# Inversion of the triangular blocks in a recurrent mixer: products spread over four quadrants of the array, transposed inverse by a product with the identity

## The chip, the cores and the metric

The kernel runs on one core of a Trainium2 chip. The metric is the device time of one launch in microseconds (us). Engines are named as the profile names them: PE (TensorE), ACT (ScalarE), DVE (VectorE), POOL (GpSimd), SP (SyncE). PSUM is the memory that PE writes, eight banks of 128 partitions by 512 fp32 numbers (`k.ps`).

## The reference, cut to what matters

The kernel computes two blocks of a network over 512 tokens. All that the change touches is inside one part of the second block, the two-directional recurrence

```
def rwkv7_scan(r, w, k, v, kk, a, reverse):
    def step(state, inp):
        sa = einsum('bhij,bhj->bhi', state, -kk_t)
        state = (state * w_t[:, :, None, :] + sa[..., None] * (kk_t * a_t)[:, :, None, :]
                 + v_t[..., None] * k_t[:, :, None, :])
        y_t = einsum('bhij,bhj->bhi', state, r_t)
```

which runs forwards and backwards for eight heads of 64 channels. The kernel does it by chunks of 64 tokens. Inside a chunk the removals (`sa`) of later tokens depend on those of earlier ones, so that a unit triangular 64x64 matrix has to be inverted for every chunk, head and direction: 8 x 8 x 2 = 128 inversions.

## The kernel before, in words

Inputs are laid out with channels or tokens on the 128 partitions. Large projections are split into high and low parts and multiplied 128x128 by 512 columns; they fill most of the time. `stage_rw_heads` (L2608) is the stage of the change. It makes four passes (`for c in range(RW_T)`), each for two heads, which lie in the lower and upper 64 partitions while channels are on the partitions. A pass does, on PE in program order: scores (L2736, 64 channels times 128 columns), transposes (`turn`, L2758), products of the scores with the values (L2788), two products for the decays and rates of the next pass (`lora`, L2711), a product of `off` with the identity that gives the transposed first level (L2799), the inversion (L2693), the inverse times `rhs` (L2833), products with `wu` (L2842, L2848, L2857, L2869), a recurrence over the eight chunks (L2879), and the output (L2892).

While tokens are on the partitions, chunk `2*it + par` stands in half `par` of the partitions (0 to 63 or 64 to 127), and a unit `u = 8*d + 4*hd + it` names direction `d`, head `hd` and pair of chunks `it`. So each tensor of the inversion (`T`, `Tt`, `Z`, `off`, 16 units of 64 columns, both halves) holds 32 matrices, 16 for each direction.

The inversion doubles the size of inverted blocks in five levels (`lv` 1 to 5; level 0 is `off` plus the identity). `T` is the inverse so far, `Tt` its transpose, and a level is, for each direction `d`:

- Z: `Z` = (score matrix) times `T`, PE; then ACT copies it out of PSUM (L2937).
- T: `Tt` times `Z`, PE; then DVE writes it into `T` where the level's mask is set (`copy_predicated`, L3130). Level 5 has none.
- Tt: `Z` times `Tt`, PE; then DVE writes it into `Tt` under the other mask (L3130).

Each of these is one call of `tiles64`, here called a product: 16 matrix multiplications of 64x64 by 64 columns into one bank. Input half and output half of the partitions are the same (`h` twice), so they use two of the four 64x64 quadrants of the array in turn. An fp32 multiplication leaves two records in the trace, so that a product has 32. A pass has 28 products. Product number `op` goes to bank `op % 8` and waits until the bank's last content is read.

The order of the work around the inversion is that of the loops, one queue for each engine, with semaphores between them (`past(engine, name, c, n)` waits for count `n` of pass `c`). Three things share the queues with it. On ACT, after the Z copy of direction 1 at levels 3, 4 and 5, three, three and four exponentials of the next pass are computed (`rw_exponentials`; the first waits for `sums`, which DVE makes at level 3); in pass 3, which has no next pass, ACT converts a weight block at level 2 (`split_hi`, L248). On DVE, ahead of the copies of each level, there is: at level 1 the centring and squaring of the pass before (`rw_spread`, L2600 to L2605, not in pass 0) and the decay scans of the next pass (`rw_scans`, L2591); at levels 2 to 5 the next pass's sums, rates and keys; in pass 3 `split_lo` (L257) at level 3. In pass 0 the attention branch's output is transposed, scaled and split among the products (`attention_turned`, `attention_high`, `attention_low`).

```
for op, (name, lv, d) in enumerate(ops):
    ...
    tiles64(pe, bank_of(op), lhs, x, d).then_inc(...)
```

## Time and profile before

| | us |
|---|---|
| median of three runs | 1899.15 |
| lowest and highest | 1898.04, 1901.95 |
| profiled execution, its time | 1899.53 |
| profiled execution, its span | 1897.8 |
| inversions, passes 0 to 3, start to the next stage's product | 29.8, 26.5, 26.6, 26.6 |

The span runs from the first to the last recorded instruction. A timeline row has the start and the length of a run of equal instructions; a matrix multiplication's record lasts about 0.22 us here although the next may start sooner, so the spacing of starts tells the rate and the length of a merged row includes one record's tail. Idle time and its releaser stand in brackets. A window row has, for each engine, the busy time in that window, and PE's granted clock as a share of 2.4 GHz.

### The profile page before, as it was taken

How to read it: one execution, taken by the hardware profiler on the slowest of the kernel's cores; microseconds unless marked ns; L12 is line 12 of the kernel's file. 1: busy time of each engine (PE TensorE's matmuls, PEld its weight loads, DVE VectorE, ACT ScalarE, POOL GpSimd, SP SyncE). 2: the span in 40 equal slices, each digit the busy share in tenths (PEclk: the TensorE clock that was granted, in tenths of full speed). 3: DMA queues.
4: the chain of work that ended last, by engine and by line, in shares of the span. 5: the costliest groups of instructions: out<-in, count | busy, mean ns of one | idle time of the engine just before them, and what ended most of it. 6: DMA issues, size and time to landing. Idle time of an engine off the chain costs nothing. (4 is left out here: it accounts for less than half of the span.)

```text
span 1897.8 us, 36848 instructions
## 1 busy us (share of the span) xinstructions
PE 1823.5 (96%) x15870; PEld 1485.6 (78%) x15870; DVE 1092.1 (58%) x1642; ACT 674.3 (36%) x1098; POOL 312.7 (16%) x296
## 2 busy tenths in 40 slices
PE   7999999999999788999999899999999999999997
PEld 6877757688888667778888669888978888888886
DVE  4665354554257788444366887787574635354545
ACT  4334332332223577442222374433233322122342
POOL 4210011130002665310021340000001000000011
PEclk9999999999999899999999999999999999999998
DMA  5334323142223110224331100002042222322231
GB/s 191 103 108 136 137 83 133 45 189 102 90 74 111 35 38 11 73 89 140 131 102 56 49 1 4 4 3 70 4 178 92 104 104 89 111 89 89 78 100 45
DMA packets 42848, 160.87 MB, mean 85 GB/s; under 512 B 5312, under 2 KB 14528, under 8 KB 28096
## 3 DMA queue, kind: packets, MB, share of 16 engines
q1 hardware_dynamic: 28480, 143.84, 22.2%
q10 hardware_dynamic: 14208, 14.68, 2.2%
q8 instruction: 126, 2.06, 0.5%
q14 instruction: 34, 0.28, 0.0%
HBM read 140.42 MB, written 16.78 MB: 83 GB/s over the span
## 5 line engine op out<-in xcount | busy, mean ns | idle before, releaser
L257 DVE TENSOR_TENSOR wlo<-raw,whi 128x2048 fp32r<-128x2048 f32 (+2 forms) x113 | 251.1, 2222 | 179.0 <-ACT whi L248 178.7
L248 ACT ACTIVATE whi<-raw 128x2048 fp32r<-128x2048 f32 (+2 forms) x113 | 209.1, 1850 | 321.4 <-PE ps L283 161.3
L281 PE MATMUL ps<-act_hi,whi 128*128 128x512 f32 x616 | 243.4, 395 | 0.0
L301 PE MATMUL ps<-act_lo,whi 128*128 128x512 f32 x632 | 240.9, 390 | 0.0
L283 PE MATMUL ps<-act_hi,wlo 128*128 128x512 f32 x616 | 240.7, 391 | 0.0
L282 PE MATMUL ps<-act_lo,whi 128*128 128x512 f32 x616 | 240.4, 390 | 0.0
L300 PE MATMUL ps<-act_hi,whi 128*128 128x512 f32 x592 | 235.5, 398 | 0.0
L305 PE MATMUL ps<-act_hi,wlo 128*128 128x512 f32 x632 | 156.5, 389 | 0.0
L301 PEld LDWEIGHTS ps<-act_lo,whi 128*128 128x128 f32 x632 | 118.7, 188 | 25.3 <-issue 1.2
L305 PEld LDWEIGHTS ps<-act_hi,wlo 128*128 128x128 f32 x632 | 118.6, 188 | 24.6
L300 PEld LDWEIGHTS ps<-act_hi,whi 128*128 128x128 f32 x592 | 111.1, 188 | 32.2 <-issue 8.1
L281 PEld LDWEIGHTS ps<-act_hi,whi 128*128 128x128 f32 x616 | 116.3, 189 | 24.4 <-issue 0.5
L283 PEld LDWEIGHTS ps<-act_hi,wlo 128*128 128x128 f32 x616 | 116.1, 188 | 24.5
L282 PEld LDWEIGHTS ps<-act_lo,whi 128*128 128x128 f32 x616 | 116.3, 189 | 24.1 <-issue 0.5
L3443 PE MATMUL ps<-f_hi,whi 128*128 128x512 f32 x256 | 99.6, 389 | 0.0
L3444 PE MATMUL ps<-f_lo,whi 128*128 128x512 f32 x256 | 99.6, 389 | 0.0
L3445 PE MATMUL ps<-f_hi,wlo 128*128 128x512 f32 x256 | 99.6, 389 | 0.0
L1838 POOL TENSOR_SCALAR att_p<-att_p,small 128x512 f32<-128x512 f32 (+3 forms) x64 | 81.9, 1280 | 52.1 <-DVE small L2005 51.1
L1938 ACT ACTIVATE att_p<-ps,small 128x512 f32<-128x512 f32 (+3 forms) x128 | 66.3, 526 | 28.5 <-DVE small L1982 28.2
L3477 DVE TENSOR_TENSOR xT<-xT,ps 128x512 f32<-128x512 f32 x32 | 22.0, 686 | 82.6 <-PE ps L3445 82.6
L3412 ACT ACTIVATE f_hi<-ff_sq 128x512 fp32r<-128x512 f32 x32 | 20.2, 633 | 123.1 <-DVE ff_sq L3468 123.1
L355 POOL TENSOR_TENSOR norm_ple_total<-norm_ple_total,norm_ple_sq 128x512 f32<-128x512 f32 x6 | 7.8, 1295 | 332.0 <-ACT norm_ple_sq L341 332.0
(552 smaller groups left out, 3478.0 us busy)
## 6 DMA issues: line engine op xcount, KB each, us to landing
raw<-stream_in SPq DMA_DIRECT2D x107, 1024.0 KB, 4.8
v_scratch<-v_out ACTq DMA_DIRECT2D x16, 256.0 KB, 3.3
z_scratch<-zt ACTq DMA_DIRECT2D x16, 256.0 KB, 3.0
mlh_v<-v_scratch SPq DMA_DIRECT2D x4, 1024.0 KB, 4.8
mlh_z<-z_scratch SPq DMA_DIRECT2D x16, 256.0 KB, 2.6
cmp_w<-cmp_w_in SPq DMA_DIRECT2D x2, 2048.0 KB, 11.3
z_scratch<-in_zt ACTq DMA_DIRECT2D x16, 256.0 KB, 3.0
mix_g<-z_scratch SPq DMA_DIRECT2D x16, 256.0 KB, 6.7
```

The source lines that it names most:

```text
L248: act.activation(k.whi[b % 2][:, 0:n], k.raw[b % RAW_SLOTS][:, 0:n], ACT.Copy).then_inc(k.hi_done, 1)
L257: dve.tensor_tensor(k.wlo[b % 2][:, 0:n], k.raw[b % RAW_SLOTS][:, 0:n], k.whi[b % 2][:, 0:n].bitcast(F32), ALU.subtract).then_inc(k.lo_don ...
L281: pe.matmul(bank, hi, x_hi, start=(x == 0), stop=False)
L282: pe.matmul(bank, hi, x_lo, start=False, stop=False)
L283: last = pe.matmul(bank, lo, x_hi, start=False, stop=(x == end))
L300: pe.matmul(bank, hi, x_hi, start=(x == 0), stop=False)
L301: pe.matmul(bank, hi, x_lo, start=False, stop=False)
L305: last = pe.matmul(bank, lo, x_hi, start=False, stop=(x == end))
L1838: pool.tensor_scalar(p[:, m % DEEP, 0, 0:L], p[:, m % DEEP, 0, 0:L], sm(32, m)[:, 0:1], None, ALU.mult) \
L3443: pe.matmul(k.ps[:, t % 4, :], whi, f_hi[:, kt, :], start=(kt == 0), stop=False)
L3444: pe.matmul(k.ps[:, t % 4, :], whi, f_lo[:, kt, :], start=False, stop=False)
L3445: last = pe.matmul(k.ps[:, t % 4, :], wlo, f_hi[:, kt, :], start=False, stop=(kt == KD - 1))
```

## The change

Three things change together in the recurrent mixer.

First, the layout. For the products of the inversion the matrices are addressed in one of two ways, `straight` (half is the chunk's parity `par`, as before) and `crossed` (half is `x`, another bit of the chunk's number). A product reads one kind and writes the other, so that its input half and output half take all four combinations, and the four combinations follow one another (`quarters`). It writes two banks, one for each input half. So that `x` and `y` fall where this needs them, the chunks of the features `ar` are stored in another order (`in_time`, `halves_together`, `place`), and several reads and writes have rearranged access patterns.

Second, `Tt` is no longer kept by a product `Z` times `Tt` and a masked copy. After each level `T` is multiplied by the identity with `T` as the stationary operand (step "R"), which gives its transpose, and ACT copies that out. At level 0 the identity times `off` goes through PSUM and DVE adds the identity, in place of a DVE addition in SBUF during the scores (L3069).

Third, the order: R(0) for both directions, then per level Z, Z, R of the level before (from level 2 on), T, T, and at the end R(5) twice: 32 products in a pass. A product waits for the reader of the one four places before it. The products after the inversion (`rhs` with `Tt`) and L2788 take rows and columns by the new places too. In the diff below the last four pieces are L2788, PE's waits (`q` is the number of the product), ACT's queue (where the exponentials still follow the Z copy of direction 1, ahead of the R copies) and DVE's.

```diff
+def in_time(a):
+    return a.rearrange("p (x m n) -> p x m n", x=2, m=4)
+def halves_together(a):
+    return a.rearrange("p (m x n) -> p x m n", x=2, m=4)
...
+    def steps_of(c):
+        out = [("R", 0, 0), ("R", 0, 1)]
+        for lv in range(1, LEVELS):
+            out += [("Z", lv, d) for d in range(2)]
+            if lv > 1:
+                out += [("R", lv - 1, d) for d in range(2)]
+            out += [("T", lv, d) for d in range(2)]
+            if c == 0 and lv < final:
+                out.append(("A", lv - 1, 0))
+        return out + [("R", final, d) for d in range(2)]
...
+    def straight(par, y, x):
+        return rows_half(par), 4 * (y // 2) + 2 * x + y % 2
+    def crossed(par, y, x):
+        return rows_half(x), 2 * y + par
+    def quarters(pe, name, lv, d, bank):
+        for y in range(4):
+            for other in range(2):
+                for source in range(2):
+                    par, x = (other, source) if name == "T" else (source, other)
+                    sh, su = straight(par, y, x)
+                    ch, cu = crossed(par, y, x)
+                    su, cu = 8 * d + su, 8 * d + cu
+                    if name == "T":
+                        to, h, lhs, y_in = sh, ch, Tt[ch, cu, :], Z[ch, cu, :]
+                    elif name == "Z":
+                        to, h, lhs, y_in = ch, sh, sc[sh, su, 0, :], T[sh, su, :]
+                    elif lv:
+                        to, h, lhs, y_in = ch, sh, T[sh, su, :], eye64[sh]
+                    else:
+                        to, h, lhs, y_in = ch, sh, eye64[sh], off[sh, su, :]
+                    last = pe.matmul(k.ps[to, bank + source, chunk(y)], lhs, y_in, start=True, stop=True)
...
-                    last = pe.matmul(k.ps[h, d, chunk(u % 8)], sc[h, u, 2, :], vtok[h, it, chunk(hd)], start=True,
-                                     stop=True)
+                    last = pe.matmul(k.ps[rows_half(it // 2), par, chunk(4 * d + 2 * hd + it % 2)], sc[h, u, 2, :],
+                                     vtok[h, it, chunk(hd)], start=True, stop=True)
...
+                    if name == "Z":
+                        past(pe, "t", c, made("T", lv - 1, d))
+                    elif name == "T":
+                        past(pe, "zc", c, made("Z", lv, d))
+                        past(pe, "rt", c, made("R", lv - 1, d))
+                    elif name == "R":
+                        past(pe, "t", c, made("T", lv, d)) if lv else past(pe, "off0", c, d + 1)
+                    if q == 1:
+                        past(pe, "t", c, 2)
+                    elif q in (2, 3) and c + 1 < RW_T:
+                        past(pe, "sigs", c + 1, 2 * q - 2)
...
+                    if name == "R" and lv:
+                        past(act, "rz", c, made(name, lv, d))
+                        act.activation(by_pair(Tt, d), from_pair(two), ACT.Copy).then_inc(ss["rt"], 1)
                     if name == "Z":
+                        past(act, "z", c, made(name, lv, d) + 2)
+                        act.activation(by_pair(Z, d), from_pair(two), ACT.Copy).then_inc(ss["zc"], 1)
...
-                past(dve, "off0", c, d + 1)
-                dve.tensor_tensor(units(Tt, d), units(off, d), eye, ALU.add).then_inc(ss["t"], 1)
...
+                    if name == "R" and lv == 0:
+                        past(dve, "rz", c, made(name, lv, d))
+                        dve.tensor_tensor(by_pair(Tt, d), from_pair(two), eye, ALU.add).then_inc(ss["rt"], 1)
                     if name == "Z":
                         if d == 0 and lv == 1 and c:
                             rw_spread(k, dve, steps, c - 1, sqr)
...
+                    if name == "T":
+                        past(dve, "tz", c, made("Z", lv, d))
+                        past(dve, "t", c, made("T", lv - 1, d))
+                        dve.copy_predicated(by_time(T, d), level_mask(lv, 1 - d).bitcast(U32),
+                                            two[:, :, 0:256].rearrange("p a (h m) -> p a h m", h=2)).then_inc(ss["t"], 1)
```

## Rows read from the trace of the kernel before

**Rows 1.** Page: busy us, share of the span and instructions of each engine.

```profile
PE 1823.5 (96%) x15870; PEld 1485.6 (78%) x15870; DVE 1092.1 (58%) x1642; ACT 674.3 (36%) x1098; POOL 312.7 (16%) x296
```

**Rows 2.** Windows: from:to, length, busy (count) of PE, PEld, DVE, ACT, POOL, clock, DMA.

```profile
1140.75:1170.55 29.80, 29.55 (x913) 28.36 (x912) 22.22 (x31) 14.75 (x26) 0.00 (x0) 1.00 0.02 5
1206.62:1233.11 26.49, 26.39 (x897) 26.25 (x897) 22.81 (x30) 12.01 (x22) 0.00 (x0) 1.00 0.02 5
...
1328.86:1355.47 26.61, 26.61 (x897) 26.39 (x897) 17.23 (x23) 7.77 (x11) 0.00 (x0) 1.00 0.02 4
```

**Rows 3.** Groups by line, 1100 to 1375 us: busy, mean ns, idle before, releaser.

```profile
L2937 ACT ACTIVATE rw_Z<-ps 128x512 f32<-128x512 f32 x40 | 23.9, 597 | 59.2 <-PE ps L2693 59.2
```

**Rows 4.** Timeline of PE in pass 1: start, length in us, instruction, idle before it.

```profile
1190.49 1.15 PE L2892 MATMUL ps<-rw_state,rw_ar 64*64 64x64 f32 x62 [0.46 <-DVE rw_state L3170]
...
1191.91 0.45 PE L2736 MATMUL ps<-rw_ar,rw_bt 64*64 64x128 f32 x8
1192.13 0.45 PE L2736 MATMUL ps<-rw_ar,rw_kt 64*64 64x128 f32 x8
...
1198.77 2.08 PE L2788 MATMUL ps<-rw_vtok,rw_sc 64*64 64x64 f32 x64
...
1212.27 2.03 PE L2693 MATMUL ps<-rw_T,rw_sc 64*64 64x64 f32 x64
1214.13 1.10 PE L2693 MATMUL ps<-rw_Z,rw_Tt 64*64 64x64 f32 x32
...
1233.11 0.27 PE L2833 MATMUL ps<-rw_rhs,rw_Tt 64*64 64x128 f32 x1
...
1237.90 0.27 PE L2848 MATMUL ps<-rw_tok,rw_wu 64*64 64x64 f32 x2
```

**Rows 5.** Timeline of DVE in pass 1.

```profile
1205.43 0.67 DVE L2600 TENSOR_REDUCE small<-rw_ytok 128x8 f32<-128x512 f32 x1
...
1208.52 2.34 DVE L2591 TENSOR_TENSOR_SCAN rw_X<-consts,rw_sig 128x512 f32<-128x512 f32 x2
1210.77 0.71 DVE L3130 COPY_PREDICATED rw_T<-rw_consts,ps 128x512 f32<-128x512 uint32 x1
1211.37 0.72 DVE L3130 COPY_PREDICATED rw_Tt<-rw_consts,ps 128x512 f32<-128x512 uint32 x1
...
1236.86 0.69 DVE L3137 COPY rw_wu<-ps 128x512 f32<-128x512 f32 x1 [0.93 <-PE ps L2833]
```

**Rows 6.** Timeline of ACT in pass 1.

```profile
1213.41 0.60 ACT L2937 ACTIVATE rw_Z<-ps 128x512 f32<-128x512 f32 x1 [4.07 <-PE ps L2693]
...
1220.56 1.28 ACT L2565 ACT_TABLE_LOAD   x1
...
1222.91 0.20 ACT L2573 ACTIVATE rw_pend<-rw_X 128x8 f32<-128x8 f32 x1
...
1226.04 0.62 ACT L2578 ACTIVATE rw_X<-rw_X 128x512 f32<-128x512 f32 x1
...
1227.08 0.62 ACT L2565 ACTIVATE rw_ar<-rw_X 128x512 f32<-128x512 f32 x1
```

**Rows 7.** Timeline of ACT in pass 3.

```profile
1337.08 1.90 ACT L248 ACTIVATE whi<-raw 128x2048 fp32r<-128x2048 f32 x1
```

**Rows 8.** Windows before, in and after stretches in which TensorE had little to do.

```profile
1075.70:1079.10 3.40, 0.07 (x2) 0.07 (x2) 2.91 (x6) 1.57 (x5) 2.78 (x3) 1.00 1.03 424
1079.10:1082.50 3.40, 3.40 (x8) 1.04 (x8) 3.33 (x5) 1.22 (x4) 3.26 (x4) 0.50 0.22 94
1249.80:1253.20 3.40, 2.03 (x78) 1.61 (x80) 1.07 (x6) 0.55 (x1) 0.00 (x0) 1.00 0.02 5
1311.20:1314.60 3.40, 2.02 (x57) 1.45 (x59) 1.15 (x7) 0.60 (x1) 0.00 (x0) 1.00 0.70 213
1314.60:1318.00 3.40, 3.40 (x96) 3.40 (x90) 1.19 (x3) 0.00 (x0) 0.00 (x0) 0.50 1.01 360
```

**Rows 9.** Timeline of PE at the start of pass 3.

```profile
1316.35 0.75 PE L2736 MATMUL ps<-rw_ar,rw_bt 64*64 64x128 f32 x8
```

More of the change, by code:

```diff
@@ L2638, in stage_rw_heads, with made, pair_of @@
     final = LEVELS - 1
-    ops = []
-    for lv in range(1, LEVELS):
-        ops += [("Z", lv, d) for d in range(2)]
-        for d in range(2):
-            ops += ([("T", lv, d)] if lv < final else []) + [("Tt", lv, d)]
-    made = {("Tt", 0, 0): 1, ("Tt", 0, 1): 2, ("T", 0, 0): 3, ("T", 0, 1): 4}
-    for x in ops:
-        if x[0] == "Z":
-            made[x] = 2 * (x[1] - 1) + x[2] + 1
-        else:
-            made[x] = 5 + sum(y in made and y[0] != "Z" for y in ops)
-    all_made = made["Tt", final, 1]
+    def steps_of(c):
[8 more added lines that the diff above has]
+        return out + [("R", final, d) for d in range(2)]
+    def made(name, lv, d):
+        return (2 * lv if name in "RT" else 2 * (lv - 1)) + d + 1
+    def pair_of(q):
+        n = 2 * (0, 2, 1, 3)[q % 4]
+        return n, k.ps[:, n:n + 2, :]
     each, ss = RW_EACH, k.rw_ss
@@ L2686, in v_of @@
         return k.rw[:, 8 + c, :]
-    def tiles64(pe, out, lhs, x, d):
-        for i in range(8):
-            for par in range(2):
-                h = rows_half(par)
-                last = pe.matmul(out[h, chunk(i)], lhs[h, 8 * d + i, :], x[h, 8 * d + i, :], start=True, stop=True)
+    def straight(par, y, x):
[19 more added lines that the diff above has]
+                    last = pe.matmul(k.ps[to, bank + source, chunk(y)], lhs, y_in, start=True, stop=True)
         return last
@@ new lines, in _ @@
+                    if q == 1:
+                        past(pe, "t", c, 2)
+                    elif q in (2, 3) and c + 1 < RW_T:
+                        past(pe, "sigs", c + 1, 2 * q - 2)
+                    elif q >= 4:
+                        held, at, side = order[q - 4]
+                        if held == "A":
+                            pe.wait_ge(daa["y_lo"], at + 1)
+                        else:
+                            past(pe, {"Z": "zc", "T": "t", "R": "rt"}[held], c, made(held, at, side))
@@ new lines, in _ @@
+                    bank, _ = pair_of(q)
+                    if name == "A":
+                        attention_turned(lv, bank)
+                    else:
+                        quarters(pe, name, lv, d, bank).then_inc(ss[{"Z": "z", "T": "tz", "R": "rz"}[name]], 1)
+                for d in range(2):
+                    past(pe, "rt", c, made("R", final, d))
+                    for y in range(4):
+                        for par in range(2):
+                            for x in range(2):
+                                h, u = crossed(par, y, x)
+                                last = pe.matmul(k.ps[rows_half(par), 2 * d + x, chunk2(y)], Tt[h, 8 * d + u, :],
+                                                 rhs[h, 8 * d + u, :], start=True, stop=True)
+                                if y == 3 and par == 1:
+                                    last.then_inc(ss["wum"], 1)
@@ L2831, in _ @@
+                places = [(d, hd, it, 8 * d + 4 * hd + it) for d in range(2) for hd in range(2) for it in range(TT)]
+                for d, hd, it, u in places:
+                    if hd == it == 0:
+                        past(pe, "wu_a", c, d + 1)
+                        past(pe, "wu_d", c, d + 1)
                     for par in range(2):
                         h = rows_half(par)
-                        last = pe.matmul(k.ps[h, u // 4, chunk2(u % 4)], Tt[h, u, :], rhs[h, u, :], start=True, stop=True)
@@ L2834, in _ @@
-                    if u % 4 == 3:
-                        last.then_inc(ss["wum"], 1)
-                places = [(d, hd, it, 8 * d + 4 * hd + it) for d in range(2) for hd in range(2) for it in range(TT)]
-                for d, hd, it, u in places:
-                    if it == 0:
-                        past(pe, ("wu_a", "wu_d")[hd], c, d + 1)
-                    for par in range(2):
-                        h = rows_half(par)
-                        last = pe.matmul(k.ps[rows_half(hd), 4 + par, chunk(4 * d + it)], wu[h, u, 0:64], sc[h, u, 1, :],
+                        last = pe.matmul(k.ps[rows_half(hd), 4 + par, chunk(4 * d + 2 * (it % 2) + it // 2)], wu[h, u, 0:64], sc[h, u, 1, :],
@@ L2945, in _ @@
                                 x()
-                for g in (0, 2):
-                    past(act, "wum", c, g + 1)
-                    act.activation(wu[:, 4 * g:4 * g + 4, :].rearrange("p u t -> p (u t)"), k.ps[:, g, :], ACT.Copy) \
+                for d in range(2):
+                    past(act, "wum", c, 2 * d + 1)
+                    act.activation(by_time(wu, d)[:, 0], k.ps[:, 2 * d, :].rearrange("p (h m) -> p h m", h=2), ACT.Copy) \
                         .then_inc(ss["wu_a"], 1)
@@ L3099, in _ @@
                         .then_inc(ss["t"], 1)
-                n = 0
-                for op, (name, lv, d) in enumerate(ops):
-                    if c == 0 and op in (9, 11, 13, 15):
-                        attention_low((op - 9) // 2)
+                for q, (name, lv, d) in enumerate(steps_of(c)):
+                    bank, two = pair_of(q)
+                    if name == "A":
+                        attention_low(lv, bank)
+                    if name == "R" and lv == 0:
+                        past(dve, "rz", c, made(name, lv, d))
+                        dve.tensor_tensor(by_pair(Tt, d), from_pair(two), eye, ALU.add).then_inc(ss["rt"], 1)
                     if name == "Z":
```

101 lines of the change are left out of this document (41 added, 60 removed).

## The prediction

> **What bounds the kernel now.** The first thing to read is the page's line of busy times: PE is busy for 96% of the span [rows 1]. A share over the whole program says little about one stage, so next I read windows around the four inversions. They last 29.8 us in pass 0 and 26.5, 26.6 and 26.6 us after it, and PE is busy in all of that while DVE is busy for 17 to 23 us and ACT for 8 to 15 [rows 2]. Third, the groups by line: in front of its 40 Z copies ACT was idle for 59.2 us, and PE's products ended all of it [rows 3]. So today readers wait for PE and PE for nobody: the inversion is bound by the issue of products. Fourth, the timeline: two products (64 records) start at 1212.27 and the next at 1214.13, so one takes 0.93 us [rows 4]; 28 of them make 26.0 us, and a level of six 5.6 us. The reader of the first product starts at 1213.41 [rows 6], 1.14 us after its start, which is 0.21 beyond its issue.
>
> **The price of a product over four quadrants.** The new order of quadrants isn't foreign to this trace. In the output product L2892, input and output halves vary together over all four: 62 records last 1.15 us, without the last one's tail 0.93 us, or 0.06 us for four [rows 4]. The scores (128 columns) start 8 records each 0.22 us [rows 4]. `tiles64` issues two in 0.06. I take half of 0.93, that is 0.47 us for a product, and 0.68 from its start to its reader's, 0.05 more where PE was idle. Bounds: 0.45, and 0.93 if the overlap fails.
>
> This is also where a rule of the Trainium skill speaks against the change. "TensorE: Matmul & The Clock Gate" (section "Wait — 56ns, not 53.3ns?") says that starts of matmuls never come closer than about 25 ns, however few columns. By it 32 records would take an estimated 0.80 us, not 0.47. The 62 records of L2892 came at 15 ns each on average [rows 4], so the trace disagrees with it here; what it would make of the time stands with the third rival.
>
> **PE's work** therefore falls from 28 x 0.93 = 26.0 to 32 x 0.47 = 15.0 us in a pass, 44 us over four. I don't forecast that, because the copies then come on the path. I follow one level of direction 0 from the start of its T copy on DVE. Prices: DVE copies last 0.73 and start 0.60 apart [rows 5]; an ACT copy lasts 0.60 [rows 6] and the next starts 0.5 later; PE starts about 0.05 after either.
> - T copied 0.73, Z(0) starts 0.79; T of direction 1 is copied at 1.33, Z(1) starts 1.39, R(0) 1.92 behind it on PE.
> - R(0)'s reader starts 2.60, copied 3.20. T(0) starts 3.25, its reader 3.98.
>
> So a bare level takes **4.0 us** against 5.6. Two kinds of other work come on top.
>
> *ACT.* The exponentials of the next pass stand after Z(1)'s copy and ahead of R(0)'s, which T(0) now waits for. Z(1)'s copy lets ACT go at 2.6, when R(0) is ready, so they add in full. Level 3: table load to the short one, 1220.56 to 1223.1, 2.55 us. Level 4: three, 0.52 apart, 1.56. Level 5: three and a short one, 1.87 [rows 6]. In pass 3 the weight block takes 1.8 at level 2 [rows 7]. Today all this lies beside PE's products.
>
> *DVE at level 1.* Counted from R(0,0)'s start, DVE's two additions run 0.68 to 1.9. Only behind them come centring (1205.43 to 1208.52, 3.09) and scans (to 1210.77, 2.25) [rows 5], and then T's copy: 7.2 us. Today centring starts while PE still works on `lora` and Z. In pass 0 there is no centring: 1.9 + 2.25 = 4.15. In pass 3 there are no scans, but R(0,1) waits 0.3 for T: 5.2. At the other levels DVE's 1.4 to 1.9 us fit between its copies, except that in pass 0 `attention_low` stands ahead of the sums and makes level 3 1.1 longer.
>
> After the T copy of level 5: 0.73, R's product 0.79 with its start, ACT 0.60 and 0.05, 2.2 us in all.
>
> | pass | levels 1 to 5, end | sum | now | difference |
> |---|---|---|---|---|
> | 0 | 4.15, 4.0, 7.7, 5.6, 5.9, 2.2 | 29.5 | 29.8 | -0.3 |
> | 1, 2 | 7.2, 4.0, 6.6, 5.6, 5.9, 2.2 | 31.5 | 26.5 | +5.0 each |
> | 3 | 5.2, 5.8, 4.0, 4.0, 4.0, 2.2 | 25.2 | 26.6 | -1.4 |
>
> In pass 3 another 0.9 goes, since the first product no longer waits for both T additions. Sum: +7.4.
>
> **Around the inversion.** L2788 (64 records, 2.08 us [rows 4]) now changes its output half every four multiplications, like L2892: half of 1.87, -0.93 a pass, -3.7. From the first L2833 to the first L2848 is 4.8 us now [rows 4]. After: direction 1's products start 0.93 behind, 1.15 to their reader, 0.69 for the copy [rows 5], then 0.35 as now (1237.55 to 1237.90): 3.1, or -1.7 a pass, -6.8. POOL's `mt`, which also waits for the last L2833, is needed only behind two more products on PE and stays hidden. The DVE addition taken out of the scores (0.7, twice a pass) I cost at nothing: PE has transposes and L2788 ahead of it there; uncovered it would be worth at most 1.2 a pass. Copies from two banks and rearranged chunks of 64 columns: no row has the same pattern; nearest, ACT copies 0.60 [rows 6], masked copies 0.72 [rows 5]. Between 0 and +0.1 for each of the ten on a pass's path, at most +4, and -0.02, -1; I take 0.
>
> So far: +7.4 - 3.7 - 6.8 = **-3.1 us**.
>
> **The clock.** After a window with PE busy for 0.07 of 3.4 us the granted clock was 0.50, that is 1.2 GHz; after one with 2.02 busy (57 records) it fell too, after one with 2.03 (78 records) it didn't [rows 8]. The inversion never idles today. Afterwards PE waits 4.7 us at level 1 of passes 1 and 2 (T(1)'s issue ends at 3.3, Z starts at 8.0), 3.0 us at level 3 of both, 4.0 at level 3 of pass 0, and about 2 at eight other levels. I expect six falls. At the low clock eight score records last 0.75 us [rows 9] against 0.45 [rows 4]; the starts are twice as far apart. With Z, Z and R in front of R's copy a level's head then loses 1.4, T another 0.4; a fall that begins inside the idle time costs less. 1.3 each, **+8**, with bounds 0 (no fall) and +15 (eight at 1.8).
>
> **Total.** -3.1 + 8 = +4.9 on the profiled execution's 1899.5 (0.4 above the median): **1904 us**.
>
> **Rivals.**
> - *The clock holds.* In a bare level PE still issues for 2.8 of 4.0 us, and one window of the recurrence with 2.03 busy held [rows 8]. Then -3.1: 1896 us. Against it: PE is idle for 4 to 5 us in three places, and after the one window of such idleness in the rows the clock was at half.
> - *The other work doesn't stand in the way*, the opposite sign. If ACT and DVE reach the R and T copies on time, a pass is 3.0 + 4 x 4.0 + 2.2 = 21.2 against 26.5, with the gains around it -7.9, four passes -32: 1868 us. It decides if exponentials or scans finish before the next product's result is there. ACT's idle time of 59.2 us speaks for it; the order of the two queues, fixed in the program, against it.
> - *The rate of starts is the limit, not the quadrants*, so that a product stays at 0.93 us. Then R(0) is read at 3.8 in its level, T(0) at 5.6, as now, and ACT, free at 3.4, adds 2.1, 1.1 and 1.4 at levels 3 to 5. Level 1 takes 8.0 and the end 2.6: passes 1 and 2 come to 8.0 + 5.6 + 7.7 + 6.7 + 7.0 + 2.6 = 37.6, +11 each. In the same way pass 0 is +6 and pass 3 +5, nothing is won around them, and the time is 1899.5 + 33 = 1932 us. Against it: L2892 [rows 4]. By the rule of the page named above (0.80 us for a product) it would be an estimated 1916 us.
> - *The clock is low for most of the inversions*, twelve falls or one that holds: +18 - 3.1, 1914 us.
>
> **How the numbers follow.** Forecast 0.42, clock holds 0.24, other work out of the way 0.12, no faster starts 0.09, low clock for long 0.13. The likeliest is 1904, by itself 1899 to 1909. A measurement here tells 0.2% from nothing, 3.8 us: the same is 1895.35 to 1902.95. Of the forecast 0.27 lies above and 0.15 inside; slower 0.27 + 0.09 + 0.13 = 0.49. Clock holds: 0.15 inside, 0.09 below; same 0.30, faster 0.09 + 0.12 = 0.21. The range leaves out the 1868 and the 1932 of two rivals (0.21 between them, but part of the second's way to it lies inside) and holds the other three: 1893 to 1914.
>
> **What would show it.** L2693's successor: 32 records with 0.47 us between the starts of two queued products (else the third rival). DVE's scans ahead of the first T copy of passes 1 and 2, with Z of level 2 about 8 us after the first R. ACT's R(2) copy right behind the short exponential, PE waiting for ACT at levels 3 to 5. Inversions of about 31.5 us in passes 1 and 2, longer than now, and 25 in pass 3, plus the clock's part. Granted clock 0.50 inside the inversions. The prediction is wrong if bare levels aren't near 4.0 us, or if the clock stays at 1.00.

## The result, and the profile after

| | us |
|---|---|
| before, median of four runs beside the changed kernel | 1898.65 (1898.04 to 1901.95) |
| after, median of four | 1921.32 (1917.83 to 1923.13) |
| ratio, 95% interval | 1.0114 [1.0095, 1.0132] |
| profiled execution after, span | 1919.1 |

The change makes the kernel 22.7 us slower. 1904 was forecast, 1893 to 1914 as the range: right in direction, wrong by 17 us. In the table of the experiments the time of e4_split is that of one run, since its other one (2047.05 us) was in the chip's slower state, with a mean granted clock of 0.965 against 0.989. The page's line of busy times, which answers to [rows 1]:

```profile
PE 1801.5 (94%) x16382; PEld 1454.4 (76%) x16382; DVE 1068.1 (56%) x1610; ACT 694.6 (36%) x1138; POOL 312.3 (16%) x296
```

PE is busy for less time and has 512 records of multiplications and 512 of weight loads more (an fp32 multiplication leaves two of each). In the kernel after, the inversion's products are L2744 (before L2693), its copies L2998 (Z), L2993 (R) and L3190 (T), `rhs` L2888, and the products with `wu` L2899, L2905 and L2914. The windows of the four inversions, from the first product of level 1 to `rhs`, answer to [rows 2]: length, busy time and count of PE, PEld, DVE, ACT and POOL, then the granted clock.

```profile
1140.51:1172.57 32.06, 23.27 (x986) 20.43 (x981) 21.13 (x28) 18.99 (x35) 0.00 (x0) 0.88 0.02 4
1209.23:1243.64 34.41, 22.10 (x972) 19.91 (x967) 21.01 (x29) 16.42 (x30) 0.00 (x0) 0.85 0.01 4
1279.10:1313.10 34.00, 22.47 (x974) 20.73 (x964) 20.72 (x29) 16.43 (x30) 0.00 (x0) 0.78 0.02 4
1346.91:1377.42 30.51, 20.77 (x970) 18.54 (x969) 12.86 (x17) 12.27 (x20) 0.00 (x0) 0.89 0.02 5
```

Together 131.0 us against 109.5 [rows 2], and the spans differ by 21.3: the loss is in these windows. What the scores' products gain in front of them, the R(0) products there take back. PE's timeline in pass 1, to compare with [rows 4] (x64 are two products):

```profile
1201.27 1.21 PE L2839 MATMUL ps<-rw_vtok,rw_sc 64*64 64x64 f32 x64
...
1209.23 1.11 PE L2744 MATMUL ps<-rw_T,rw_sc 64*64 64x64 f32 x64
1210.59 1.18 PE L2744 MATMUL ps<-rw_Z,rw_Tt 64*64 64x64 f32 x64 [0.25 <-ACT rw_Z L2998]
1216.32 1.99 PE L2744 MATMUL ps<-rw_T,rw_sc 64*64 64x64 f32 x64 [4.54 <-DVE rw_T L3190]
1218.08 1.74 PE L2744 MATMUL ps<-rw_consts,rw_T 64*64 64x64 f32 x64
1219.92 1.36 PE L2744 MATMUL ps<-rw_Z,rw_Tt 64*64 64x64 f32 x64
1221.46 1.38 PE L2744 MATMUL ps<-rw_T,rw_sc 64*64 64x64 f32 x64 [0.18 <-DVE rw_T L3190]
1222.65 1.11 PE L2744 MATMUL ps<-rw_consts,rw_T 64*64 64x64 f32 x62
1224.74 0.32 PE L2744 MATMUL ps<-rw_consts,rw_T 64*64 64x64 f32 x2 [0.98 <-issue]
1226.64 1.99 PE L2744 MATMUL ps<-rw_Z,rw_Tt 64*64 64x64 f32 x64 [1.58 <-issue]
```

Three things are to be seen. Two products that wait for nothing take 1.11 us with the last one's tail: without it 0.9, so 0.45 each, the price that was forecast (0.47). PE then idles for 4.5 us at level 1, behind DVE's queue, also as forecast, and the next products (1216.32, 1218.08) are stretched by the half clock. The third is new: at 1224.74 PE stops for 0.98 us two records before the end of a product, with no wait on anything ("issue"). (The 1.58 in the row below it is no such stop: at 1226.57 ACT finished the R copy that this product reads, the one behind the exponentials.) Pass 3 has six such stops, 5.4 us of idle time in all. Its last four:

```profile
1364.18 0.46 PE L2744 MATMUL ps<-rw_Z,rw_Tt 64*64 64x64 f32 x16 [1.35 <-issue]
1364.46 0.65 PE L2744 MATMUL ps<-rw_T,rw_sc 64*64 64x64 f32 x32
1365.49 0.69 PE L2744 MATMUL ps<-rw_T,rw_sc 64*64 64x64 f32 x32 [0.38 <-DVE rw_T L3190]
1366.01 0.87 PE L2744 MATMUL ps<-rw_consts,rw_T 64*64 64x64 f32 x46
1367.89 0.50 PE L2744 MATMUL ps<-rw_consts,rw_T 64*64 64x64 f32 x17 [1.01 <-issue]
...
1371.99 0.51 PE L2744 MATMUL ps<-rw_T,rw_sc 64*64 64x64 f32 x18 [0.82 <-issue]
...
1375.49 0.51 PE L2744 MATMUL ps<-rw_Z,rw_Tt 64*64 64x64 f32 x19 [0.81 <-issue]
```

Count the records of multiplications from one stop to the next: 16 + 32 + 32 + 46 = 126, and in each of the other two intervals 126 as well. Each has the record of its weight load, which makes 252 instructions, and a few that wait or signal. Over all four windows the stops lie whole multiples of 126 apart (give or take a missing record), though not every multiple has one. The page's queues show what comes in pieces of that size, 16 KB each:

```profile
q8 instruction: 130, 2.13, 0.5%
```

That is 64 bytes for each of 256 instructions. The stops stand 3.71, 4.10 and 3.50 us apart. PE has used up its instructions and waits for the next 256. The times of the packets bear this out: PE restarts at 1364.18, a packet runs from 1365.41 to 1366.50, and PE, stopped in the meantime, restarts at 1367.89. The round takes 1.23 + 1.09 + 1.39 = 3.71 us. The inversions of all the kernels in the table below have 147 stops, and every one ends 1.2 to 1.6 us after such a packet has landed. Between neighbouring stops no packet sets out sooner than 1.15 us after PE has resumed.

One multiplication of 64x64 by 64 columns in fp32 is four PE instructions (two loads, two multiplications), a product of 16 multiplications is 64, and a pass went from 28 products (1792) to 32 (2048). The kernel before ran 1792 in 26.5 us, 3.79 us for 256 [rows 2]: about as fast as the kernel after is fed. Its trace already has one stop in the inversions, 0.32 us from start to start at 1232.88, the very end of pass 1, and it too ends 1.5 us after a packet.

This bears on the Trainium skill. "Runtime: NRT & Kernel Launch" (section "Instruction fetch mechanics") says that instructions are fetched in 16 KiB blocks of 256, and that the fetch is hidden because the engine issues more slowly than it is filled. The blocks are as the page has them; the rest isn't so here: products that could issue 64 instructions in 0.45 us, 256 in 1.8, were held to some 3.8.

### The profile page after: what moved, and what is told of

It is laid out like the page before. It is cut to its first block and busy times, and to the rows that moved or that the text cites. A ratio compares the mean times of both kernels' runs of the same rounds, so it can differ in the third digit from the quotient of the medians.

```text
span 1919.1 us, 37863 instructions
## 1 busy us (share of the span) xinstructions
PE 1801.5 (94%) x16382; PEld 1454.4 (76%) x16382; DVE 1068.1 (56%) x1610; ACT 694.6 (36%) x1138; POOL 312.3 (16%) x296
## 5 line engine op out<-in xcount | busy, mean ns | idle before, releaser
L301 PEld LDWEIGHTS ps<-act_lo,whi 128*128 128x128 f32 x632 | 120.3, 190 | 25.8 <-issue 1.2
L1838 POOL TENSOR_SCALAR att_p<-att_p,small 128x512 f32<-128x512 f32 (+3 forms) x64 | 81.7, 1278 | 52.6 <-DVE small L2005 51.6
L1938 ACT ACTIVATE att_p<-ps,small 128x512 f32<-128x512 f32 (+3 forms) x128 | 66.4, 526 | 29.2 <-DVE small L1982 29.0
```

What stands on the lines that cost most here:

```text
L301: pe.matmul(bank, hi, x_lo, start=False, stop=False)
L1838: pool.tensor_scalar(p[:, m % DEEP, 0, 0:L], p[:, m % DEEP, 0, 0:L], sm(32, m)[:, 0:1], None, ALU.mult) \
```

## The experiments

Theory S (supply): 256 PE instructions take at least some 3.8 us (single blocks 3.4 and more), whatever they do. Theory C (chain): only the array, the copies and the order of ACT's and DVE's queues count. Theory K: the clock's falls cost what was forecast for them. In the table, "stops" are distances over 0.3 us from one PE start to the next, inside the four inversions, without a wait and not beside 512 columns; "low" is the time at 1.2 GHz there; the inversions go from the first product of level 1 to `rhs`.

| kernel | median us | ratio to before [95%] | inversions us | stops us | low us |
|---|---|---|---|---|---|
| before | 1898.65 | | 29.9, 26.5, 26.6, 26.6 | 0.3 | 0 |
| after | 1921.32 | 1.0114 [1.0095, 1.0132] | 32.1, 34.4, 34.0, 30.5 | 15.4 | 40 |
| e1_wide | 1909.91 | 1.0056 [1.0040, 1.0073] | 28.9, 33.0, 33.5, 25.8 | 0 | 34 |
| e2_transposes | 1912.71 | 1.0068 [1.0053, 1.0083] | 31.6, 37.2, 33.2, 24.8 | 1.6 | 47 |
| e3_order | 1907.12 | 1.0040 [1.0028, 1.0052] | 28.2, 30.4, 29.6, 29.2 | 26.7 | 3 |
| e3a_spread | 1916.80 | 1.0103 [1.0087, 1.0118] | 31.3, 33.3, 31.4, 29.9 | 14.1 | 29 |
| e3b_exps | 1909.26 | 1.0059 [1.0046, 1.0073] | 27.9, 32.5, 30.2, 27.5 | 22.9 | 14 |
| e4_split (one run) | 1999.90 | 1.053, no interval | 55.2, 52.6, 52.5, 52.7 | 0.4 | 0 |
| e5_both | 1891.08 | 0.9959 [0.9945, 0.9972] | 23.9, 29.0, 27.6, 24.2 | 9.6 | 7 |
| e6_warm | 1919.80 | 1.0116 [1.0103, 1.0130] | 31.7, 35.0, 34.0, 30.6 | 23.4 | 1 |
| e7_many | 1941.75 | 1.0238 [1.0221, 1.0255] | 34.3, 38.9, 40.7, 38.0 | 10.9 | 78 |
| e8_one | 1887.92 | 0.9947 [0.9933, 0.9961] | 25.2, 27.5, 25.3, 27.2 | 3.0 | 3 |
| e9_warm2 | 1906.74 | 1.0049 [1.0036, 1.0062] | 28.9, 33.2, 30.8, 24.6 | 3.3 | 3 |
| e10_half | 1904.89 | 1.0035 [1.0023, 1.0047] | 28.7, 29.0, 28.8, 30.1 | 16.1 | 1 |
| e11_bwide | 1893.22 | 0.9967 [0.9955, 0.9980] | 28.7, 24.8, 24.8, 24.8 | 0 | 0 |

The kernel before ran beside each group, at 1897.6 to 1899.2 us.

**e1_wide: the kernel after with half the instructions.** Each multiplication takes two neighbouring units' 128 columns (so the inverses aren't the reference's).

```diff
-        for y in range(4):
+        for y in (0, 2):
...
-                    ... Tt[ch, cu, :], Z[ch, cu, :]
+                    ... Tt[ch, cu, :], Z[ch, cu:cu + 2, :]
```

> The changed kernel, with each two multiplications of a product in the inversion replaced by one of 128 columns (8 instead of 16 in a product, same columns in all, same quadrants, same order and waits). The second 64 columns are multiplied with the first one's stationary matrix, so the inverses are wrong; only the time is meant. Theory S (supply): PE is short of instructions, since a product is 64 of them (32 weight loads, 32 multiplications) and gaps of 0.5 to 1.2 us stand in the middle of products with no wait at them. Half the instructions take most of these gaps away: 8 to 15 us less than the changed kernel's 1921, that is 1906 to 1913. Theory C (chain and clock only): array time and waits are unchanged, so within 3 us of 1921.

1909.91 us: 11 us by the ratios come back with the same columns, order and queues, and every stop is gone. In the windows of passes 1 and 3 the counts are half of those after:

```profile
1203.65:1236.66 33.01, 20.30 (x490) 16.76 (x482) 20.42 (x29) 16.48 (x31) 0.00 (x0) 0.84 0.01 2
1337.49:1363.33 25.84, 19.88 (x488) 15.96 (x480) 12.46 (x17) 12.41 (x21) 0.00 (x0) 0.87 0.01 3
```

Pass 3, where little else stood in the way, gains most (30.5 to 25.8). Its levels 4 and 5, which have no other work in them, now take 4.11 and 4.04 us from T copy to T copy, against 6.32 and 5.58 in the kernel after: the bare level of 4.0 us that the prediction counted on exists, but only with half the instructions.

**e2_transposes: R by four transposes of 128x128.** 8 PE instructions in place of 64. Units of T are stored in another order for it, and R(0) now transposes T, so that DVE copies its result instead of adding the identity.

```diff
+        if name == "R":
+            for y in range(4):
+                u = 8 * d + 2 * y
+                last = pe.transpose(k.ps[:, bank, P * y:P * y + P], T[:, u:u + 2, :]..., k.const("ident"))
+            return last
```

> The changed kernel, with step R (also that of level 0, now from T) made by four 128x128 transposes with the identity instead of 16 multiplications of 64x64: 8 PE instructions instead of 64, about the same PE time (four transposes issue in 0.5 us in the trace, a product in 0.47). T's units are stored in another order for it. Same waits. Theory S: 12 x 56 = 672 PE instructions less in a pass of 2048, so a third of the gaps go and less is late: 5 to 12 us less than 1921, 1909 to 1916. Theory C: PE time as before, within 3 us of 1921.

1912.71 us, inside S's range. Nearly all stops are gone here too. But PE's idle time outside the stops grows from 30.7 to 35.5 us over the four inversions, and the low clock from 40 to 47 us.

**e3_order: what stands ahead of the copies.** On DVE the centring and squaring (`rw_spread`) goes ahead of R(0)'s additions; on ACT the exponentials and pass 3's weight block go behind the two R copies that they stood ahead of.

```diff
+                if c:
+                    rw_spread(k, dve, steps, c - 1, sqr)
...
-                        if d == 0 and lv == 1 and c:
-                            rw_spread(k, dve, steps, c - 1, sqr)
...
                         act.activation(by_pair(Z, d), from_pair(two), ACT.Copy).then_inc(ss["zc"], 1)
-                        if d == 1 and lv == 2 and c + 1 == RW_T:
+                    if name == "R" and d == 1:
+                        if lv == 1 and c + 1 == RW_T:
                             split_hi(k, act, b0)
-                        if d == 1 and c + 1 < RW_T:
-                            if lv == 3:
+                        if c + 1 < RW_T:
+                            if lv == 2:
                                 past(act, "sums", c + 1, 1)
-                            for x in steps[slice(*{3: (0, 3), 4: (3, 6), 5: (6, 10)}.get(lv, (0, 0)))]:
+                            for x in steps[slice(*{2: (0, 3), 3: (3, 6), 4: (6, 10)}.get(lv, (0, 0)))]:
                                 x()
```

> The changed kernel, with two things moved in the queues: on DVE the centring of the pass before (3.1 us) ahead of the additions of R(0), while PE still works on the lora products; on ACT the exponentials and the weight block behind the R copies of the level before, instead of ahead of them. Theory C: the level-1 wait of passes 1 and 2 falls by 3.1 us each and of pass 3 by 1.5, the exponentials (6 us a pass in passes 0 to 2) cost some 2 us instead, and with shorter waits two or three clock falls go: 20 to 25 us less than 1921, 1896 to 1901. Theory S: PE can't be fed 2048 instructions faster than some 29 us a pass, so no more than about 8 to 12 us go, 1909 to 1913.

1907.12 us, between the two ranges: the order is worth 14 us by the ratios. PE's idle time outside the stops falls from 30.7 to 17.6 us and the clock is at 2.4 GHz for all but 3 us, but the stops rise from 15.4 to 26.7 us. The inversion of pass 1:

```profile
1200.94:1231.36 30.42, 18.35 (x973) 16.30 (x967) 19.23 (x26) 16.13 (x30) 0.00 (x0) 1.00 0.02 4
```

PE is busy for 18.4 of 30.4 us, the chain is shorter, and it is still slower than before (26.5), at 4.0 us for 256.

**e3a_spread and e3b_exps: its two parts alone.** The first two pieces of the diff above (`rw_spread`) are e3a_spread, the third is e3b_exps.

> The changed kernel with only the centring of the pass before moved ahead of the additions of R(0) on DVE. By the chain: 3.1 us at level 1 of passes 1 and 2, 1.5 in pass 3, and the falls behind the idle 4.7 us: 8 to 10 us less, 1911 to 1913. If supply hides it (PE would have waited for instructions anyway): 3 us or less.

> The changed kernel with only ACT's exponentials and weight block moved behind the R copies of the level before. By the chain: 4 us a pass in passes 0 to 2 and 1 to 2 in pass 3, less some clock, so 8 to 14 us less, 1907 to 1913. If supply hides it: 3 us or less.

1916.80 and 1909.26 us. The ACT part is worth 10 us by the ratios, as the chain had it. The DVE part is worth 2, which the intervals don't tell from nothing and which was expected only if supply hides it. The exponentials in front of the R copies were the costlier of the two. Why the DVE part gave so little was not followed further; its low clock is still 29 us.

**e4_split: the kernel before with twice the instructions.** Every multiplication is done in two halves of 32 columns.

```diff
-                last = pe.matmul(out[h, chunk(i)], lhs[h, 8 * d + i, :], x[h, 8 * d + i, :], ...)
+                for w in range(2):
+                    a = slice(32 * w, 32 * w + 32)
+                    last = pe.matmul(out[h, 64 * i + 32 * w:64 * i + 32 * w + 32], lhs[h, 8 * d + i, :],
+                                     x[h, 8 * d + i, a], ...)
```

> The kernel before, with each multiplication of the inversion split into two of 32 columns with the same stationary matrix: twice the instructions for the same columns, result unchanged. Theory S: 28 x 64 = 1792 more PE instructions a pass; the trace fetches 256 at a time, one fetch about every 3.5 to 3.9 us at best, so +25 us a pass, about +100, 2000 us, in bursts with gaps between them. If the limit is the array's time for the columns: some 0.06 us per two records stays 0.03 per two of half the length, and the time stays within 10 us of 1899. If it is an even spacing of starts of 29 ns, also about 2000 us but without gaps.

1999.90 us, as S had it, and as an even spacing of starts would have it. The window of pass 1:

```profile
1230.86:1283.50 52.64, 52.49 (x1791) 52.38 (x1792) 23.33 (x30) 12.52 (x22) 0.00 (x0) 1.00 0.02 5
```

The same columns take twice as long: 3583 instructions in 52.64 us, 3.76 for 256, the same rate as before. But the starts are evenly spaced, with a single stop (0.4 us) in four inversions, so a limit of two quadrants on loads or starts would look the same, and is the likelier here. Taken alone this run doesn't decide; the rate agrees with S. It does show the size of a packet: 7168 PE records more than in the kernel before, and 154 packets in place of 126, which is 256 instructions each.

**e5_both: fewer instructions and the better order.** The diffs of e2_transposes and e3_order together.

> Transposes for step R and the moved order together, on the changed kernel. In the run with the order alone the granted clock stays at 1.00 in all inversions, but 34 us of gaps without a wait are left in the middle of products; with the transposes alone these are 6.5 us and the clock falls in every pass. If supply and waits are two causes that add, the gaps and the falls both go: 1907 less 8 to 12, 1895 to 1899, level with the kernel before or a little under it. If the transposes gave their 9 us by something else that the order also gives, it stays near 1905.

1891.08 us, 0.9959 [0.9945, 0.9972]: faster than both kernels. The two edits gave 0.0046 and 0.0074 of the time alone and 0.0155 together; the excess, 0.0035 or some 7 us, is not far beyond the intervals' widths. (The expectation's 34 and 6.5 us of gaps are from a wider count than the table's stops.) The counts of stops and waits say why there should be one. Each alone runs into what the other removes: the shorter chain into the supply, the smaller number of instructions into the chain.

**e6_warm: no low clock.** Where PE waits long, products of 512 columns with the identity keep it at work.

```diff
+                        for _ in range(n_fill):
+                            pe.matmul(k.ps[:, pair_of(q)[0], :], k.const("ident"), k.const("cos", S), ...)
```

> The changed kernel with products of a constant by the identity (512 columns, 0.86 us each, four PE instructions) put in where PE waits: four ahead of Z of level 2 in passes 1 and 2, two or three ahead of T of level 3, one ahead of T of levels 4 and 5, two in pass 3. They write banks that the next product overwrites; the result is unchanged. If the clock falls cost what I put on them (about 1.3 us for each 3.4 us at half clock, and some 48 us of the inversions are at half clock), 10 to 16 us go: 1905 to 1911, with the granted clock at 1.00 in nearly all of the inversions. If the clock costs little because PE is idle or short of instructions anyway: within 4 us of 1921.

```profile
1210.07:1245.08 35.01, 26.38 (x990) 19.35 (x981) 20.82 (x29) 16.22 (x30) 0.00 (x0) 0.98 0.01 4
1281.39:1315.37 33.98, 25.99 (x986) 18.87 (x981) 20.83 (x29) 16.22 (x30) 0.00 (x0) 1.00 0.01 3
```

The clock is back at 0.98 and 1.00, from 0.85 and 0.78, and the two inversions take 35.0 and 34.0 us, as long as after. What the array gained the stops took: 15.4 us became 23.4.

**e9_warm2: the same where instructions aren't short.** The diff of e6_warm on top of e2_transposes, with the same numbers of products in the same places.

> e2_transposes (1360 PE instructions an inversion, 47 us of the four inversions at half clock) with products of 512 columns with the identity in PE's long waits, as in e6_warm. It asks what the low clock costs where PE isn't short of instructions. If the clock matters there (theory K): the half clock goes from some 47 us to under 10, and each fall gives back about 1 us, so 1903 to 1908 us in place of 1912.7. If the falls cost nothing, as e6_warm showed for the changed kernel (theory N): 1910 to 1914 us.

1906.74 us, inside K's range. Beside the kernel before it is 0.0019 of the time, or 3.6 us, faster than e2_transposes, and the two intervals overlap, so the times alone don't show a gain. In the profiled executions the four inversions lose 9.3 us (e9_warm2's was the fastest of its five, e2_transposes' the second slowest of its four). That the low clock has a price where supply isn't in the way is likely, and its size open.

**e7_many and e8_one: instructions against array time.** Both are e5_both with extra work ahead of PE's wait for the first T product of each level: 56 multiplications of one column, or one of 512 columns.

```diff
+                            for z in range(56):
+                                pe.matmul(k.ps[rows_half(z % 2), pair_of(q)[0] + z // 2 % 2, 0:1],
+                                          eye64[rows_half(z // 2 % 2)], eye64[rows_half(z // 2 % 2), 0:1], ...)
```

and for e8_one in its place

```diff
+                            pe.matmul(k.ps[:, pair_of(q)[0], :], k.const("ident"), k.const("cos", S), ...)
```

> e5_both with 56 multiplications of one column each (64x64, fp32, going round the four quadrants; 112 PE instructions) put ahead of PE's wait for the first T product of every level: 560 more PE instructions in an inversion, 1920 in place of 1360, as many as the changed kernel and e3_order have. Their array time is about 0.85 us a level, in a place where PE waits for ACT's R copy. Supply theory (S): 256 PE instructions cost at least some 3.8 us wherever they stand, so the inversions go back to those of e3_order (28.2, 30.4, 29.6, 29.2 us against 23.9, 29.0, 27.6, 24.2), with starts inside products late by 0.5 to 1.2 us and no wait named: e5_both's 1891 us + 12.6 = 1904 us, 1900 to 1909. Array and wait theory (C, only times in the array and the waits between engines count): 0.85 us beside a wait, 0 to 0.3 us a level, 1891 to 1897 us.

> The control to e7_many: e5_both with one multiplication of 512 columns (about 0.85 us in the array, 2 to 8 PE instructions) in the same places, ahead of PE's wait for the first T product of every level. Supply theory (S): no instructions to speak of are added, so the time is that of e5_both, 1889 to 1896 us, and e7_many is 8 to 15 us slower than this kernel. Array and wait theory (C): the same as e7_many within 2 us.

1941.75 us, outside both ranges, against 1887.92, 1 us under S's range. The number of added instructions was twice what the text expected (four for each multiplication, as elsewhere, not two): 2480 in an inversion, which took 34.3 to 40.7 us, 3.5 to 4.2 for 256. Their array time was 1.6 us a level against the control's 0.95, and the clock was low for 78 us, so the 54 us between the two kernels are not supply alone. Therefore once more with half of them.

**e10_half: 28 multiplications of one column.** Now their time in the array (0.80 us) is under the control's (0.95).

```diff
-                            for z in range(56):
+                            for z in range(28):
```

> e7_many put twice the PE instructions in that its text said, since one fp32 multiplication is four PE instructions here and not two (224 a level, 1120 an inversion, 1.62 us when unhindered). This kernel has 28 one-column multiplications instead of 56 ahead of each level's first T product: 112 PE instructions, some 0.81 us a level, against e8_one's 0.95 us in the same places; 1920 PE instructions an inversion, as in the changed kernel and e3_order, against 1380 in e8_one. Supply theory (S): at the 3.7 us for 256 instructions that e7_many kept to, an inversion takes at least 27.8 us and, with its own idle time on top, that of e3_order (28.2 to 30.4), so 1898 to 1909 us, 10 to 20 us over e8_one's 1887.9. Array and wait theory (C): at or below e8_one, 1885 to 1890 us.

1904.89 us, 17 us over e8_one by the ratios, with no more array time in the same places; S had 10 to 20, C none. The windows of pass 1, first e10_half, then e8_one:

```profile
1203.53:1232.48 28.95, 22.71 (x961) 19.74 (x961) 18.61 (x26) 16.54 (x30) 0.00 (x0) 1.00 0.02 5
```

```profile
1201.14:1228.62 27.48, 22.25 (x692) 16.46 (x691) 18.55 (x26) 16.34 (x31) 0.00 (x0) 1.00 0.01 3
```

PE, DVE and ACT are nearly as busy in the one as in the other, and the clock is full in both. The difference is 539 instructions. Over the four inversions, 11.4 us longer in e10_half, PE's idle time outside the stops is the same (11.0 and 11.1 us); that of the stops is 12.7 against 2.0. e10_half's timeline has the stops in products that weren't changed, and again 126 records apart (15 + 8 + 56 + 47):

```profile
1226.61 0.46 PE L2749 MATMUL ps<-rw_T,rw_sc 64*64 64x64 f32 x15 [1.09 <-issue]
1227.00 1.09 PE L2734 MATMUL ps<-consts,rw_T 128*128 128x128 f32 x8
1228.02 0.99 PE L2874 MATMUL ps<-rw_consts 64*64 64x1 f32 x56
1228.86 0.90 PE L2749 MATMUL ps<-rw_Z,rw_Tt 64*64 64x64 f32 x47
1230.57 0.50 PE L2749 MATMUL ps<-rw_Z,rw_Tt 64*64 64x64 f32 x17 [0.81 <-issue]
```

56 records of one column, 8 of 128 and 62 of 64 are another mix of work for the array than 126 of 64, and the stop still comes after 126 of them and their loads. This pair shows the supply limit. e8_one is the fastest kernel that ran, 0.9947 [0.9933, 0.9961]; from e5_both (0.9959) it isn't told apart.

**e11_bwide: was the kernel before at the limit already?** Its products of 8 multiplications with 128 columns each (neighbouring units share their weights, so the inverses aren't the reference's).

```diff
-        for i in range(8):
+        for i in range(0, 8, 2):
...
+                y = x[h, 8 * d + i:8 * d + i + 2, :]
```

> The kernel before with each product of tiles64 made of 8 multiplications of 128 columns instead of 16 of 64 (neighbouring units share their weights, so the inverses and what follows from them are not the reference's): half the PE instructions, the same columns, everything else as it was. If the kernel before is held by the columns in its two quadrants (theory A), a product stays at 0.85 to 0.93 us and the inversions at 24.5 to 26.6 us: 1890 to 1898 us. If it is already held by the supply of instructions (theory S2: 64 instructions for 0.93 us is 256 for 3.7 us), the products get faster than 0.85 us: the inversions fall below 24 us and the time below 1888 us.

```profile
1206.77:1231.61 24.84, 24.84 (x450) 24.26 (x449) 22.64 (x30) 11.77 (x21) 0.00 (x0) 1.00 0.01 3
```

24.8 us in place of 26.5, 1893.22 us: theory A, inside its range. With half the instructions a product still takes 0.87 us, so the columns in two quadrants held the kernel before to no less than 24.8 us a pass. What set the other 1.7 us is not shown: the pace of starts in two quadrants, or the supply, which allows about that rate (3.8 us for 256 is 0.95 for 64) and shows in the one stop at 1232.88. In either case the two limits lay close together. Removing the first while adding 14% to the number of instructions could win next to nothing in the inversion.

## Why the prediction was wrong

**The steps that held.** A product over four quadrants: 0.45 to 0.47 us while nothing holds it up; with it the third rival (no faster starts, 1932 us) falls. By the rule of the Trainium skill's "TensorE: Matmul & The Clock Gate" (section "Wait — 56ns, not 53.3ns?"), 25 ns between starts, two products would take an estimated 1.6 us; the 64 records at 1209.23 took 1.11, so the trace disagrees with it. L2788's successor L2839: 1.21 us for 64 records against 2.08 in [rows 4], the 0.9 a pass that was forecast. With the 0.9 of pass 3, what stands in front of the four inversions came to -4.5 us, as forecast (-3.7 and -0.9). DVE at level 1: in pass 1 from the start of the first R(0), 1208.25, to the T copy 7.3 us (7.2 forecast):

```profile
1213.31 2.34 DVE L2603 TENSOR_TENSOR_SCAN rw_X<-consts,rw_sig 128x512 f32<-128x512 f32 x2
1215.57 1.31 DVE L3190 COPY_PREDICATED rw_T<-rw_consts,ps 128x512 f32<-128x512 uint32 x2
```

The exponentials ahead of R's copies, level 3 of pass 1:

```profile
1223.52 1.28 ACT L2576 ACT_TABLE_LOAD   x1
1224.81 0.63 ACT L2576 ACTIVATE rw_ar<-rw_X 128x512 f32<-128x512 f32 x1
1225.35 0.61 ACT L2581 ACTIVATE rw_E<-rw_E 128x512 f32<-128x512 f32 x1
1225.87 0.20 ACT L2585 ACTIVATE rw_pend<-rw_X 128x8 f32<-128x8 f32 x1
1225.97 1.06 ACT L2993 ACTIVATE rw_Tt<-ps 128x512 f32<-128x512 f32 x2
```

2.45 us from the table load to the R copy, 2.55 forecast, and e3b_exps shows that it is on the path. The second rival (other work out of the way, 1868 us) falls with it. To take that work out of the way is nevertheless worth something: e3_order is 14 us faster than the kernel after.

**The step that failed: PE's work "falls from 28 x 0.93 = 26.0 to 32 x 0.47 = 15.0 us in a pass", with nothing else between PE and its products, and from it the bare level of 4.0 us.** The sum priced a product by the array (0.47 us) and by the waits between engines. That 64 instructions also have to be delivered, and that [rows 2] already had 1794 of them in 26.49 us, was in no term and no rival. In pass 3, where the prediction had three bare levels of 4.0 us at the end, they took 5.24, 6.32 and 5.58; that is its own sign of being wrong. With half the instructions (e1_wide) the last two are back at 4.11 and 4.04. The error in two places:

- The inversions, from R(0): forecast 29.5, 31.5, 31.5 and 25.2, with 8 for the clock 125.7 us in all. Measured 33.1, 35.4, 35.0 and 32.4 (in pass 1 from 1208.25 to 1243.64), 135.9. **+10.2 us.** e1_wide, which only halves the instructions, takes 9.8 of that back in the windows of the table; the biggest miss, pass 3 (25.2 against 32.4), is where the forecast left PE the least time to wait.
- From the first L2833 to the first L2848: 4.8 to 3.1 us, -6.8 in all. Measured 4.83, 3.76, 4.42 and 3.92 us, -2.2 in all, and the products behind them, up to the output's, took 2.6 more than before, with stops of their own:

```profile
1249.97 0.22 PE L2914 MATMUL ps<-rw_wu,rw_tok 64*64 64x64 f32 x1
1250.70 0.27 PE L2914 MATMUL ps<-rw_wu,rw_tok 64*64 64x64 f32 x2 [0.51 <-issue]
```

  **+7.2 us.** In e1_wide the stretch takes 3.50 in every pass, so 2.9 of it is the supply, left short by the inversion in front. What the rest behind the inversion is, is open; dense products there have such a stop in the kernel before too (0.38 us at 1241.18).

10.2 + 7.2 = 17.4 us. The spans of the two profiled executions differ by 21.3 us, which is 16.4 more than the 4.9 of the forecast; the other 1.0 came back elsewhere, most of it behind the last pass.

**The clock.** Six falls at 1.3 us were forecast. There were nine, 40 us at 1.2 GHz inside the four windows, so the fourth rival's condition (low for long) came true, and the time is nearest to its 1914. But its price didn't: e6_warm took the low clock away and the time stayed within the noise (1919.80 us). One of the stretches, and the idle window in front of it:

```profile
1212.90:1216.30 3.40, 0.00 (x0) 0.00 (x0) 3.37 (x5) 0.00 (x0) 0.00 (x0) 0.96 0.00 0
1216.10:1219.50 3.40, 3.18 (x120) 3.19 (x124) 2.48 (x4) 1.47 (x3) 0.00 (x0) 0.51 0.02 5
```

244 instructions in 3.4 us at half clock is 3.6 us for 256, hardly faster than what the supply gives at full clock. So the two limits hide each other, and the 8 us of the sum were, in the kernel after, the same microseconds as the supply's, as far as e6_warm tells: it gained nothing. The first rival (clock holds, 1896 us) is refuted twice: it didn't hold, and held up by e6_warm it gives 1920.

## What to carry to other kernels

Before you make PE's small products cheaper in the array, divide the PE instructions of the stage (here four for each fp32 multiplication) by its time: at 256 in some 3.8 us the stage was, in this kernel, already at what the instruction queue delivers, and a faster product only turns into stops marked "issue". Cut instructions first: wider multiplications, or four transposes of 128x128 in place of sixteen multiplications of 64x64 with the identity. And try both edits together, since a shortened chain and a shortened instruction stream can hide each other's gain (9 and 14 us alone here, 29 together).

## What the runs showed of the hardware

- PE's instructions arrive 256 at a time, 16 KB in one packet (28 packets for 7168 instructions, e4_split). Where PE uses them faster it stops, in the kernel after for 0.4 to 1.4 us of idle time, at a multiple of 252 records, wherever in a product that falls. Whole inversions ran at 3.5 to 4.2 us for 256 (e7_many), 3.76 (e4_split) and 3.8 to 4.0 (e10_half).
- A packet took 0.9 to 1.5 us, set out at the earliest 1.15 us after PE had resumed, and PE resumed 1.2 to 1.6 us after it had landed (147 stops in 13 kernels). These three add up to the distance of neighbouring stops (3.71 us from 1364.18 on).
- Waits of PE take the place of stops: in pass 1 a block of the kernel after ends at 1218.09, behind the wait of 4.5 us at level 1, without a stop, and e3_order, with its waits shortened, has 26.7 us of stops against 15.4. How much is held ready was not measured.
- Multiplications over four quadrants start on average 14 ns apart (64 records in 1.11 us less a tail of 0.22), and with one column instead of 64 no closer: 56 records in 0.8 us, 14 ns.
- Halving the columns of a 64x64 fp32 multiplication in two quadrants saved nothing (e4_split: twice as many, in 52.6 us against 26.5); doubling them, with half as many, took 0.87 us a product against 0.93 (e11_bwide).
- The clock fell to 1.2 GHz not only after the idle time of 4.5 us (low at 1216.1) but also around one of 1.6 us (low at 1226.3). In the kernel after, taking the low clock away (e6_warm) gained no time that could be measured.
